# First expert's input by one-hot matmuls, and the third down-projection load behind the second expert's gather

## The chip, the core and the metric

The kernel runs on one core of one Trainium2 chip. The metric is the device time of one execution in microseconds. Engines are named as in the profile: PE is TensorE's matmuls, PEld its weight loads, DVE is VectorE, ACT is ScalarE, POOL is GpSimd, SP is SyncE, and SPq stands for the DMA issues of SP.

## What is computed

Two layers over 512 tokens of width 1024. Each layer is a mixer (attention and retention, then `w_out`) followed by a mixture of 32 experts, two per token; one RMSNorm ends the kernel. The part that matters is the mixture:

```python
g_idx = jnp.argmax(g_logits, axis=-1)              # one of 4 groups per token
top_v, top_i = lax.top_k(e_in_group, K)            # 2 of its 8 experts
eid = (g_idx[:, None] * EXPERTS_PER_GROUP + top_i).reshape(-1)
...
def expert_block(args):
    xblk, e = args
    a = jax.nn.silu(xblk @ w_expert_gate[e]) * (xblk @ w_expert_up[e])
    return a @ w_expert_down[e]
...
out = jax.ops.segment_sum(yb * w_buf[:, None], tok_buf, num_segments=N)
```

Each expert has a gate, an up and a down matrix of 1024x512 or 512x1024 in float32, 2 MB each. All of them are read once per layer, whatever the routing says.

## The kernel before

The 512 tokens are four tiles of 128 rows (`t` = 0 to 3, `NT` = 4). Each expert takes 64 slots (`SLOTS`); a slot holds one token. Rows that do not fit go through further blocks at the layer's end. Each of five engines (SP, POOL, ACT, DVE, PE) runs a program of its own, and semaphores order them. A list of steps (`steps`, line 166) fixes the order in which PE, ACT and DVE go through the mixer and the router; each keeps to that order.

**The end of the mixer and the router.** Step `wo` adds the mixer's output to the residual `xres` (L1320). ACT then takes the sum of squares of the tile (`rstd`, L782, its square at L784). `fT` transposes the tile on PE (L1637), DVE copies it out (L1331), and `lg` makes the 36 router logits (L1644, out of PSUM at L1341). `ffn_rows` (L1015, the multiplication at L1017) writes the normalised tile `xn2[t % 2]` on DVE; for the last tile this comes right behind the last `fT` copy. POOL stores each normalised tile to a DRAM buffer `rows` (L724). `route` (L1069) is a chain of small DVE operations: the choice of the experts (up to L1084), then the rank of each token in its expert, a matmul of PE (steps `rank`, L1651 and L1654), then one-hots of the slots (`hot_slot`, L1100), the weights of the choices (`weigh`, L1052), and, after the matmuls of step `table` (L1455), the list of row numbers `gath` (L1049). `wtab` (L1462) makes the weight of each slot.

**The gathers.** POOL waits for that list and for the four stores, and then issues one indirect DMA per expert (`gather`, L733), which brings the expert's 64 rows into one of three buffers `xg[e % 3]`. The first three go out in a row, each further one as soon as its buffer was transposed.

**The experts.** For each expert PE transposes the gathered rows (L1679), DVE multiplies them by the norm's weight into `xT` (`take_input`, L1351), PE multiplies by gate and up (L1711), ACT applies SiLU, DVE the product (L1354), PE transposes that (L1720), DVE copies it (L1374), PE multiplies by down (L1727), and two more steps (`y_hi`, `y_lo`) and a spreading matmul (L1687) add the result to the residual (L1120). Weights lie in three slots (`RING`). SP issues their loads in one order: expert 3's gate goes out when expert 0's gate matmuls are done, its up after expert 0's up, its down after expert 0's down (`load_expert`, L649), and so on to expert 31. The first three experts are loaded ahead. The last of these nine loads, the down matrix of expert 2, waits in SP's program for the first gather to land (L646):

```python
sp.wait_ge(s_gat[0], 16 * (layer * len(range(0, NE, 3)) + 1))
load_down(layer, 2, 2)
```

and everything that SP issues later, expert 3's gate first, stands behind that wait. `unread` (L1799) is a matmul whose result nobody reads.

## Time and profile before

| | |
|---|---|
| median of 3 runs | 1539.42 us (1537.19 to 1541.54) |
| span of the profiled execution | 1538.5 us; the median lies 0.9 us above it |
| PE busy | 1471.8 us, 96% |
| DVE busy | 822.5 us, 53% |
| ACT, POOL busy | 342.0 us (22%), 262.3 us (17%) |
| mean granted TensorE clock | 0.983 |
| DMA | 464.30 MB, mean 302 GB/s |

The two layers lie one behind the other: mixer and router of layer 0 up to about 306 us, its experts to about 770 us, then the same again. How the page is read: the busy time of an engine is a sum over stages with different limits, so the 96% of PE does not say that PE sets the end. The slices show where DMA is full:

```profile
## 2 busy tenths in 40 slices
PE   8999999799999999998999999996999999999996
...
PEclk9999999799999999999999999997999999999998
DMA  6442144799999999999833321448999999999995
GB/s 205 103 97 69 42 164 178 271 400 423 423 423 421 424 421 423 423 423 424 333 116 95 82 69 28 166 195 350 423 423 422 424 420 425 421 424 421 424 423 228
```

One slice is 38.5 us. In some twenty of the slices, both expert stages, the DMA engines move about 423 GB/s.

### The profile page before, as it was taken

The page shows a single profiled execution, that of the slowest core. Times are in us where ns is not written, and L with a number is a line of the kernel's source. Part 1 is how long each engine was busy: PE and PEld are TensorE (multiplying, and loading weights), DVE is VectorE, ACT ScalarE, POOL GpSimd, SP SyncE. Part 2 cuts the span into 40 slices and gives each one's busy share as a digit, 9 for nine tenths or more (in the row PEclk, how much of TensorE's full clock was granted, in tenths as well). Part 3 has the DMA queues.
Part 4 walks back from the last instruction along what each step waited for, and adds up shares of the span by engine and source line. Part 5 has one row for each costly group of instructions (what it writes and reads, how often), then busy time and mean ns, then how long its engine had stood idle before and what let it go on. Part 6 is the DMA issues. An engine that isn't in the chain of part 4 may idle for free.

```text
span 1538.5 us, 23362 instructions
## 1 busy us (share of the span) xinstructions
PE 1471.8 (96%) x9302; PEld 930.0 (60%) x9302; DVE 822.5 (53%) x1518; ACT 342.0 (22%) x682; POOL 262.3 (17%) x155
## 2 busy tenths in 40 slices
PE   8999999799999999998999999996999999999996
PEld 6877768655555555544488777685555555554443
DVE  2267774545555555454534586635455555555446
ACT  6335463100000000000163354710000000000002
POOL 3343332100000000000133332401000000000001
PEclk9999999799999999999999999997999999999998
DMA  6442144799999999999833321448999999999995
GB/s 205 103 97 69 42 164 178 271 400 423 423 423 421 424 421 423 423 423 424 333 116 95 82 69 28 166 195 350 423 423 422 424 420 425 421 424 421 424 423 228
DMA packets 105932, 464.30 MB, mean 302 GB/s; under 512 B 16706, under 2 KB 59970, under 8 KB 72800
## 3 DMA queue, kind: packets, MB, share of 16 engines
q1 hardware_dynamic: 98208, 449.13, 73.1%
q0 software_dynamic: 6272, 12.60, 2.2%
q8 instruction: 77, 1.26, 0.3%
q10 hardware_dynamic: 1344, 1.05, 0.2%
q14 instruction: 31, 0.25, 0.0%
HBM read 464.84 MB, written 6.29 MB: 306 GB/s over the span
## 4 chain that ended last, share of the span: by engine, by line
PE 78%; DMA 17%; DVE 3%; issue 1%; ACT 0%; DVEq 0%; ACTq 0%; POOLq 0%
PE bank L1711 23%; DMA area<-in_w_expert_up_dram 16%; PE bank L1727 11%; PE bank L1687 7%; PE bank L1559 5%; PE bank L1564 5%; PE bank L1563 5%; PE bank L1629 2%; PE bank L1631 2%; PE bank L1487 2%; PE bank L1630 2%; PE bank L1488 2%; PE bank L1489 2%; PE bank L1579 2%; PE bank L1601 1%; DVE area L1374 1%
## 5 line engine op out<-in xcount | busy, mean ns | idle before, releaser
L1711 PE MATMUL bank<-area 128*64 128x256 f32 x4096 | 464.0, 383 | 19.1 <-DMA area<-in_w_expert_up_dram 16.8
L1711 PEld LDWEIGHTS bank<-area 128*64 128x64 f32 x4096 | 289.1, 138 | 189.0 <-issue 27.3
L1120 DVE TENSOR_TENSOR xres<-xres,bank 128x512 f32<-128x512 f32 x512 | 316.4, 679 | 5.2 <-PE bank L1687 5.2
L1727 PE MATMUL bank<-area 128*64 128x512 f32 x1024 | 233.8, 598 | 6.0 <-DVE area L1374 1.0
L734 POOL DMA_INDIRECT area<-rows,gath x64 | 72.0, 1125 | 746.5 <-PE bank L1679 714.7
L1354 DVE TENSOR_TENSOR area<-area,bank 128x256 f32<-128x256 f32 x64 | 27.0, 421 | 293.3 <-PE bank L1711 293.3
L708 POOL TENSOR_TENSOR w_lo<-area,w_hi 128x1024 fp32r<-128x1024 f32 x55 | 135.1, 2459 | 274.6 <-ACT w_hi L806 274.6
L970 ACT ACTIVATE y_hi<-bank,slot_w 128x512 fp32r<-128x512 f32 x64 | 44.1, 688 | 576.7 <-PE bank L1727 576.7
L1727 PEld LDWEIGHTS bank<-area 128*64 128x64 f32 x1024 | 67.8, 136 | 130.8 <-issue 109.6
L1559 PE MATMUL bank<-h_hi,w_hi 128*128 128x512 f32 x336 | 135.0, 402 | 0.0
L1564 PE MATMUL bank<-h_hi,w_lo 128*128 128x512 f32 x320 | 124.9, 390 | 0.0
L1563 PE MATMUL bank<-h_lo,w_hi 128*128 128x512 f32 x320 | 124.7, 390 | 0.0
L1687 PE MATMUL bank<-y_hi,onehot 64*128 64x512 f32 x512 | 115.6, 446 | 3.0 <-issue 1.6
L1687 PE MATMUL bank<-y_lo,onehot 64*128 64x512 f32 x512 | 102.5, 394 | 0.0
L1687 PEld LDWEIGHTS bank<-y_hi,onehot 64*128 64x128 f32 x512 | 48.4, 184 | 83.5 <-issue 75.8
L966 ACT ACTIVATE area<-bank 128x256 f32<-128x256 f32 x64 | 24.6, 385 | 278.2 <-PE bank L1711 278.2
L1358 DVE SCALAR_TENSOR_TENSOR y_lo<-bank,slot_w,y_hi 128x512 fp32r<-128x512 f32 x64 | 48.0, 750 | 69.9 <-ACT y_hi L970 69.9
L806 ACT ACTIVATE w_hi<-area 128x1024 fp32r<-128x1024 f32 x58 | 61.6, 1062 | 84.0 <-PE bank L1489 32.7
L1559 PEld LDWEIGHTS bank<-h_hi,w_hi 128*128 128x128 f32 x336 | 63.0, 188 | 22.9 <-issue 10.3
L1564 PEld LDWEIGHTS bank<-h_hi,w_lo 128*128 128x128 f32 x320 | 60.1, 188 | 13.0
L1563 PEld LDWEIGHTS bank<-h_lo,w_hi 128*128 128x128 f32 x320 | 60.1, 188 | 11.5
L1374 DVE COPY area<-bank 128x256 f32<-128x256 f32 x64 | 27.2, 425 | 68.6 <-PE bank L1720 68.6
(186 smaller groups left out, 1662.1 us busy)
## 6 DMA issues: line engine op xcount, KB each, us to landing
area<-in_w_expert_up_dram SPq DMA_DIRECT2D x64, 2048.0 KB, 27.4
area<-in_w_expert_gate_dram SPq DMA_DIRECT2D x64, 2048.0 KB, 25.8
area<-in_w_expert_down_dram SPq DMA_DIRECT2D x64, 2048.0 KB, 26.6
area<-in_w_in_dram SPq DMA_DIRECT2D x58, 512.0 KB, 3.9
area<-in_w_out_dram SPq DMA_DIRECT2D x4, 2048.0 KB, 11.1
rows<-area POOLq DMA_DIRECT2D x8, 512.0 KB, 6.2
area<-in_decay_dram SPq DMA_DIRECT2D x2, 1024.0 KB, 6.2
out_dram<-area SPq DMA_DIRECT2D x4, 512.0 KB, 2.9
```

The source lines that it names most:

```text
L708: nc.gpsimd.tensor_tensor(w_lo[g % CUT][:, :, :], slab[g % RAW], w_hi[g % CUT][:, :, :].bitcast(F32), ALU.subtract).then_inc(s_wlo, 1)
L734: pool.indirect_dma_start(out=xg[e % 3], out_offset=None, in_=rows_dram, in_offset=bass.IndirectOffsetOnAxis(ap=gath[:, e:e + 1], axis=0), ...
L806: nc.scalar.activation(w_hi[g % CUT][:, :, :], slab[g % RAW], ACT.Copy).then_inc(s_whi, 1)
L970: nc.scalar.activation(y_hi[e % 2][:, :], bank[3][:, :], ACT.Copy, scale=slot_w[:, e:e + 1]).then_inc(s_yh, 1)
L1120: tt(xs, xs, bank[4 + i][:, :], ALU.add).then_inc(s_sa[i], 1)
L1358: return nc.vector.scalar_tensor_tensor(out=y_lo[e % 2][:, :], in0=bank[found][:, :], scalar=weight, in1=y_hi[e % 2][:, :].bitcast(F32), o ...
L1559: mm(o[:, :], hi[:, c, :], h_hi[:, c, :], start=(c == 0), stop=False)
L1563: mm(o[:, :], hi[:, c, :], h_lo[:, c, :], start=False, stop=False)
L1564: last = mm(o[:, :], lo[:, c, :], h_hi[:, c, :], start=False, stop=(c == KC - 1))
L1687: yield mm(bank[4 + 2 * (t % 2) + half][:, :], onehot[parity][rows, P * t:P * (t + 1)], part[rows, :], start=(w_ == 0), stop=(w_ == 1))
L1711: last = mm(bank[i][SLOTS * half:SLOTS * (half + 1), 0:256], xT[:, c % 4, c // 4, :], w[:, i, c, 256 * half:256 * (half + 1)], start=(c == ...
L1727: last = mm(bank[into][SLOTS * half:SLOTS * (half + 1), :], hx[:, c % 2, c // 2, :], w[:, c, 512 * half:512 * (half + 1)], start=(c == 0), ...
```

## The change

The input of the first expert of each layer no longer comes by a gather. All four normalised tiles are kept in SBUF (`XN0` has four places, and the buffers of the expert stage are laid out around them). Once the ranks are known DVE makes a one-hot per tile for expert 0 (`hot_first`), and PE multiplies it with the kept tiles in a new step `xb`, 8 calls of float32 matmuls. DVE waits for all four stores to land, copies the result to `xg[0]` in two halves, and PE transposes it (`first_transpose`). The gathers begin at expert 1. The list of row numbers is made around the first transposes: 3 matmuls ahead of them, 5 behind; DVE takes the list out of PSUM after it has made expert 0's `xT`. The matmuls of the slot weights move behind expert 0's up matmuls, the weights' DVE work and `further` likewise move into expert 0.

The last normalised tile is written by ACT instead of DVE, after the last logits are complete. ACT no longer waits for a store ahead of the tiles 2 and 3, and its squares go to another scratch place. PE gets `unread` matmuls of 2816 columns in all behind the last `lg`. On SP the down matrix of expert 2 waits for the gather of expert 1.

```diff
@@ -66,15 +66,15 @@
-XN0 = PT0
-XG0 = PB0
-XT0 = XG0 + 3 * 512
-SG0 = XT0 + 512
+XN0 = (PT0, PT0 + D, PB0, PB0 + D)
+YH0 = PB0
+XT0 = YH0 + 4 * 512
+OH0 = XT0 + 512
+SG0 = OH0 + 2 * T
-YH0 = HX0 + 256
-OH0 = YH0 + 4 * 512
-assert PLEN <= (RH - 1) * T and OH0 + 2 * T <= AREA and DK0 + RH * T <= 2 * EXPERT and KT0 + FH * T <= EXPERT
+XG0 = HX0 + 256
+assert PLEN <= (RH - 1) * T and XG0 + 3 * 512 <= AREA and XN0[1] + D <= CS0 and DK0 + RH * T <= 2 * EXPERT and KT0 + FH * T <= EXPERT
...
@@ -224,7 +224,7 @@
-    out += [("fT", 3, 1), ("lg", 3, 1), ("rank",), ("table",), ("wtab",)]
+    out += [("fT", 3, 1), ("lg", 3, 1), ("rank",), ("xb",), ("table",), ("wtab",)]
...
@@ -525,6 +527,11 @@
+        def gathered(layer, e):
+            count = [len(range(i or 3, NE, 3)) for i in range(3)]
+            return 16 * (layer * count[e % 3] + e // 3 + (e % 3 > 0))
...
@@ -641,9 +648,7 @@
-                sp.wait_ge(s_gat[0], 16 * (layer * len(range(0, NE, 3)) + 1))
+                sp.wait_ge(s_gat[1], gathered(layer, 1))
...
@@ -721,14 +726,13 @@
-                    pool.dma_start(dst, xn2[t % 2].rearrange("p (h n) -> p h n", h=2)).then_inc(s_rows[t % 2], 16)
-                pool.wait_ge(s_ret, RH * (layer + 1))
-                nc.gpsimd.memset(at(XG0, 3 * 512), 0.0).then_inc(s_xgz, 1)
+                    pool.dma_start(dst, xn2[t].rearrange("p (h n) -> p h n", h=2)).then_inc(s_rows[t], 16)
+                nc.gpsimd.memset(at(XG0 + 512, 2 * 512), 0.0).then_inc(s_xgz, 1)
-                for i in range(2):
-                    pool.wait_ge(s_rows[i], 16 * (NT // 2) * (layer + 1))
+                for t in range(NT):
+                    pool.wait_ge(s_rows[t], 16 * (layer + 1))
...
@@ -736,7 +740,7 @@
-                for e in range(RING):
+                for e in range(1, RING):
...
@@ -940,10 +944,14 @@
-                        if t >= 2:
-                            act.wait_ge(s_rows[t % 2], 16 * (layer * (NT // 2) + t // 2))
-                        rstd(xres[:, t, :], t, xn2[t % 2], s_rstd2)
+                        rstd(xres[:, t, :], t, at(CS0, D), s_rstd2)
+                    elif kind == "lg" and s[1:] == (NT - 1, 1):
+                        t = s[1]
+                        act.wait_ge(s_rstd2, layer * NT + t + 1)
+                        is_full(act, s[:2], layer)
+                        nc.scalar.activation(xn2[t].rearrange("p (h j q) -> p h j q", h=2, j=4),
+                                             xres[:, t, :].rearrange("p (q h j) -> p h j q", h=2, j=4), ACT.Copy,
+                                             scale=stat[:, 16 + t:17 + t]).then_inc(s_xn2, 1)
...
@@ -958,8 +966,6 @@
-                act.wait_ge(s_tab, layer + 1)
...
@@ -1094,20 +1100,24 @@
+                link(nc.vector.tensor_copy(rank_first, rank[:, :, 0]))
+                for t in range(NT):
+                    ts(hot_first[:, t, :], k("slot")[:, 0:SLOTS], rank_first[:, t:t + 1],
+                       chosen[:, t, 0:1].bitcast(F32), ALU.is_equal, ALU.mult).then_inc(s_first_hot, 1)
-                weigh(layer)
-                b, n = result(("table",), layer)
-                rows_of(layer, ("table",), 0, NE).then_inc(freed[b], 1)
-                for i in range(2):
-                    dve.wait_ge(s_rows[i], 16 * (NT // 2) * (layer + 1))
-                is_taken(dve, ("table",), layer)
-                dve.sem_inc(s_tab, 1)
+                for t in range(NT):
+                    dve.wait_ge(s_rows[t], 16 * (layer + 1))
+                b, n = result(("xb",), layer)
+                is_full(dve, ("xb",), layer)
+                for half in range(2):
+                    own = slice(256 * half, 256 * (half + 1))
+                    nc.vector.tensor_copy(xg[0][:, own], bank[b][:, own]).then_inc(freed[b], 1)
...
@@ -1330,8 +1340,6 @@
-                        if t == NT - 1 and half:
-                            ffn_rows(layer, t)
...
@@ -1370,11 +1378,17 @@
+                    if e == 0:
+                        slot_weights(layer)
+                    if e == 0:
+                        is_taken(dve, ("table",), layer)
+                    if e == 0:
+                        further(layer)
...
@@ -1390,9 +1404,10 @@
-                slot_weights(layer)
-                further(layer)
+                b, n = result(("table",), layer)
+                rows_of(layer, ("table",), 0, NE).then_inc(freed[b], 1)
+                weigh(layer)
...
@@ -1462,6 +1477,10 @@
+            def unread(b, *widths):
+                for n in widths:
+                    mm(bank[b][:, 0:n], ident, kst[:, 0:n], start=True, stop=True)
...
@@ -1654,12 +1673,13 @@
-                    elif kind == "table":
-                        pe.wait_ge(s_tabin, layer + 1)
-                        last = table(o, hot_exp, NE, TOPK * layer)
-                    elif kind == "wtab":
-                        pe.wait_ge(s_wtin, layer + 1)
-                        last = weight_table(o[:, 0:NE], hot_w)
+                    elif kind == "xb":
+                        pe.wait_ge(s_xn2, NT * (layer + 1))
+                        for t in range(NT):
+                            pe.wait_ge(s_first_hot, NT * layer + t + 1)
+                            for half in range(2):
+                                last = mm(o[SLOTS * half:SLOTS * (half + 1), :], hot_first[:, t, :],
+                                          xn2[t][:, 512 * half:512 * (half + 1)], start=(t == 0), stop=(t == NT - 1))
...
@@ -1670,11 +1690,35 @@
-                pe.wait_ge(s_tab, layer + 1)
+                    if s == ("lg", NT - 1, 1):
+                        is_taken(pe, ("lg", NT - 2), layer)
+                        unread(2, 512, 512, 512, 512, 512, 256)
+                def slots_by_expert(part):
+                    b, n = result(("table",), layer)
+                    if part[0] == 0:
+                        may_fill(pe, ("table",), layer)
+                        pe.wait_ge(s_tabin, layer + 1)
+                    last = table(bank[b], hot_exp, NE, TOPK * layer, part)
+                    if part[-1] == TOPK * NT - 1:
+                        last.then_inc(full[b], 1)
+                def weights_by_expert():
+                    b, n = result(("wtab",), layer)
+                    may_fill(pe, ("wtab",), layer)
+                    pe.wait_ge(s_wtin, layer + 1)
+                    weight_table(bank[b][:, 0:NE], hot_w).then_inc(full[b], 1)
+                def first_transpose():
+                    b, n = result(("xb",), layer)
+                    for j in range(4):
+                        if j % 2 == 0:
+                            pe.wait_ge(freed[b], 2 * n - 1 + j // 2)
+                        last = tr(bank[0][:, P * j:P * (j + 1)], xg[0][:, P * j:P * (j + 1)], ident)
+                    last.then_inc(s_xtf, 1)
-                    pe.wait_ge(s_gat[e % 3], 16 * (layer * per(e % 3) + e // 3 + 1))
+                    pe.wait_ge(s_gat[e % 3], gathered(layer, e))
...
@@ -1742,6 +1786,8 @@
+                    if e == 0:
+                        weights_by_expert()
...
@@ -1760,7 +1806,9 @@
-                input_transpose(0)
+                slots_by_expert(range(0, 3))
+                first_transpose()
+                slots_by_expert(range(3, TOPK * NT))
```

## Rows read from the trace of the kernel before

**Rows 1.** Chain of waits, in order of time: start us, us, what.
```profile
602.18 7.08 PE bank L1711 x64
609.28 40.09 DMA area<-in_w_expert_up_dram
```
**Rows 2.** Busy time by stretch, for DMA: window, length, busy per engine, clock, DMA share, GB/s.
```profile
600.00:700.00 100.00, 93.32 (x694) 50.58 (x692) 48.91 (x86) 7.51 (x14) 6.86 (x6) 1.00 1.01 423
...
313.30:315.70 2.40, 2.40 (x26) 1.57 (x24) 1.82 (x5) 0.38 (x1) 0.00 (x0) 1.00 0.66 137
...
1071.80:1074.00 2.20, 2.20 (x24) 1.44 (x22) 1.81 (x5) 0.38 (x1) 0.00 (x0) 1.00 0.76 164
```
**Rows 3.** Timeline of SP, both layers: start us, us, issue.
```profile
305.77 0.38 SPq L595 DMA_DIRECT2D area<-in_w_expert_down_dram  x1
313.64 0.33 SPq L587 DMA_DIRECT2D area<-in_w_expert_gate_dram  x1
...
1064.28 0.38 SPq L595 DMA_DIRECT2D area<-in_w_expert_down_dram  x1
1071.78 0.33 SPq L587 DMA_DIRECT2D area<-in_w_expert_gate_dram  x1
```
**Rows 4.** DMA issues of rows 3, same order, last number us to landing.
```profile
area<-in_w_expert_down_dram SPq DMA_DIRECT2D x1, 2048.0 KB, 9.0
area<-in_w_expert_gate_dram SPq DMA_DIRECT2D x1, 2048.0 KB, 8.9
...
area<-in_w_expert_down_dram SPq DMA_DIRECT2D x1, 2048.0 KB, 8.7
area<-in_w_expert_gate_dram SPq DMA_DIRECT2D x1, 2048.0 KB, 7.8
```
**Rows 5.** The stores of L724: the one at 291.67 us, and all eight.
```profile
rows<-area POOLq DMA_DIRECT2D x1, 512.0 KB, 9.8
...
DMA to landing us min/median/max: 3.2/6.2/10.2
```
**Rows 6.** Timeline of DVE, both layers.
```profile
290.22 1.14 DVE L1017 TENSOR_SCALAR area<-xres,stat 128x1024 f32<-128x1024 f32 x1 [0.23 <-ACT stat L791]
...
298.58 1.29 DVE L1100 TENSOR_TENSOR hot_slot<-kst,area 128x512 fp32r<-128x512 f32 x2
...
301.32 0.25 DVE L1049 TENSOR_SCALAR gath<-bank,kst 128x32 int32<-128x32 f32 x1 [0.30 <-PE bank L1455]
...
301.58 0.42 DVE L1108 COPY area<-nfe 128x512 f32<-128x512 f32 x1
...
307.01 0.69 DVE L1351 TENSOR_TENSOR area<-bank,area 128x512 f32<-128x512 f32 x1 [1.96 <-PE bank L1679]
...
1059.60 0.25 DVE L1049 TENSOR_SCALAR gath<-bank,kst 128x32 int32<-128x32 f32 x1 [0.29 <-PE bank L1455]
```
**Rows 7.** Timelines of ACT and POOL, layer 0.
```profile
288.48 1.06 ACT L784 ACTIVATE area<-xres 128x1024 f32<-128x1024 f32 x1 [14.71 <-DVEq L1324]
...
291.67 0.72 POOL L724 DMA_DIRECT2D rows<-area  x1 [5.27 <-DVE area L1017]
```
**Rows 8.** Timeline of PE, layer 0; last row: L1801's matmul durations, min/median/max ns.
```profile
290.05 1.08 PE L1644 MATMUL bank<-rtw,area 128*128 128x36 f32 x8 [0.88 <-DVE area L1331]
...
318.62 3.65 PE L1727 MATMUL bank<-area 128*64 128x512 f32 x16
...
L1801 PE MATMUL bank<-kst x8: 379/434/697, 765.4 to 771.1; 128*128 128x256 f32 x4, 128*128 128x512 f32 x2, 128*128 128x384 f32 x2
```
**Rows 9.** Busy time by stretch, for the clock: columns as in rows 2, PE first.
```profile
287.61:291.13 3.52, 1.71 (x12) 1.39 (x12) 2.37 (x4) 1.65 (x4) 0.00 (x0) 1.00 1.00 343
291.13:296.40 5.27, 0.01 (x1) 0.02 (x1) 4.58 (x23) 0.00 (x0) 2.12 (x2) 0.55 0.97 405
307.76:312.18 4.42, 4.42 (x22) 2.53 (x24) 3.97 (x14) 0.00 (x0) 1.00 (x1) 0.50 0.96 398
1049.38:1054.70 5.32, 0.00 (x0) 0.03 (x1) 4.63 (x23) 0.00 (x0) 2.12 (x2) 0.51 0.99 415
```

More of the change, by code:

```diff
@@ L272, in banks @@
             b = 5
+        elif kind == "xb":
+            b = 3
         elif kind == "table":
@@ L365, in trunk_kernel @@
         hT2 = [at(PB0 + i * D, D).rearrange("p (c t) -> p c t", c=KC) for i in range(2)]
-        xn2 = [at(XN0 + i * D, D) for i in range(2)]
+        xn2 = [at(start, D) for start in XN0]
         wexp = [(at(s * EXPERT, 2 * KC * DE).rearrange("p (g c n) -> p g c n", g=2, c=KC),
@@ L414, in trunk_kernel @@
         pick = rt(2, TOPK, NT)
+        rank_first = rt(NT)
+        hot_first = rt(NT, SLOTS)
         cmp_st = rt(TOPK * NT, MAXBLK - 1)
@@ L462, in trunk_kernel @@
         s_gate = sem("gate_done")
-        s_sd = sem("decayed_scores_ready")
         s_sq = sem("retention_square_ready")
@@ L469, in trunk_kernel @@
         s_xn2 = sem("ffn_xn_ready")
-        s_rows = [sem(f"rows{i}_saved") for i in range(2)]
+        s_rows = [sem(f"rows{i}_saved") for i in range(NT)]
         s_rtw = sem("router_weights_scaled")
@@ L477, in trunk_kernel @@
         s_hots = sem("one_hots_of_slots_ready")
-        s_tab = sem("tables_ready")
+        s_first_hot = sem("first_expert_one_hots_ready")
         s_wtin, s_wt = sem("slot_weight_one_hots_ready"), sem("slot_weights_ready")
@@ L482, in trunk_kernel @@
         s_more = sem("further_tables_ready")
-        s_wb = sem("ffn_weight_spread")
         s_w = [[sem(f"slot{s}_{n}_loaded") for n in ("gate", "up", "down")] for s in range(RING)]
@@ L1016, in ffn_rows @@
                 dve.wait_ge(s_rstd2, layer * NT + t + 1)
-                ts(xn2[t % 2].rearrange("p (h j q) -> p h j q", h=2, j=4),
+                ts(xn2[t].rearrange("p (h j q) -> p h j q", h=2, j=4),
                    xres[:, t, :].rearrange("p (q h j) -> p h j q", h=2, j=4), stat[:, 16 + t:17 + t], None, ALU.mult
@@ L1447, in _, with table @@
             ident = k("ident")
-            def table(o, hot_col, n, ready=None):
-                for i in range(TOPK * NT):
+            def table(o, hot_col, n, ready=None, part=range(TOPK * NT)):
+                for i in part:
                     if ready is not None and i % NT == 0:
@@ L1495, in _ @@
                     kind = s[0]
-                    if kind in ("gate", "mh", "ml", "ws", "rs") or kind == "fv" and s[1] < 3:
+                    if kind in ("gate", "mh", "ml", "ws", "rs", "table", "wtab") or kind == "fv" and s[1] < 3:
                         continue
@@ L1656, in _ @@
                                       start=False, stop=(u == NT))
-                    elif kind == "table":
-                        pe.wait_ge(s_tabin, layer + 1)
-                        last = table(o, hot_exp, NE, TOPK * layer)
-                    elif kind == "wtab":
-                        pe.wait_ge(s_wtin, layer + 1)
-                        last = weight_table(o[:, 0:NE], hot_w)
+                    elif kind == "xb":
+                        pe.wait_ge(s_xn2, NT * (layer + 1))
[4 more added lines that the diff above has]
+                                          xn2[t][:, 512 * half:512 * (half + 1)], start=(t == 0), stop=(t == NT - 1))
                     if kind == "PV":
@@ L1797, in _ @@
                                 pe.wait_ge(o["added_half"], j * 2 + (part + 1))
-                def unread(b, *widths):
-                    for n in widths:
-                        mm(bank[b][:, 0:n], ident, kst[:, 0:n], start=True, stop=True)
                 if layer + 1 < DEPTH:
```

## The prediction

> **What bounds the kernel now.** I read the slices first, for where DMA is full, then the chain of waits, then the windows at the edges of the full stretch, and last the timelines of the five engines around the router. PE's 96% tempts one to call PE the bound. The chain says something finer: about 22 experts long it runs over PE alone, and from 609.28 us it runs over the loads of the up matrices [rows 1]. From there PE waits for weights. DMA is at full share, 423 GB/s, in that stretch [rows 2], and the slices show the same rate from the first experts on. So the expert stage of a layer ends when one uninterrupted stream of loads ends. At 423 GB/s a 2 MB load takes 4.96 us and an expert 14.9 us, more than PE needs: 7.08 us for gate and up, 3.65 us for down [rows 1, 8] and some 3 us for spreads and transposes. PE starts with three experts loaded ahead and uses that lead up.
>
> The consequence decides this case. **What PE gains at the start of the experts is worth nothing by itself; only an earlier stream is.** The stream of expert 3 to 31 cannot begin before two things in SP's program: the down matrix of expert 2, which waits for a gather, and expert 3's gate, which stands behind it and waits for expert 0's gate matmuls. They were issued at 305.77 and 313.64 us in layer 0, at 1064.28 and 1071.78 us in layer 1 [rows 3]. Between them the stream has a hole: the down matrix landed at 305.77 + 9.0 = 314.8 us, the gate matrix at 313.64 + 8.9 = 322.5 us [rows 4], 7.7 us apart where 4.96 us is the full rate. The hole is 2.7 us by that and (423 - 137) / 423 x 2.4 = 1.6 us by the window [rows 2]; I take 2.2 us. In layer 1 the landings are 1073.0 and 1079.6 us, a hole of 1.6 us, and 1.35 us by the window [rows 2, 4]; I take 1.5 us. The change can win back at most these holes, 3.7 us in both layers, as far as the down matrix is not issued later.
>
> **The change, part by part.** Layer 0, all of it on the way to that issue.
>
> 1. *The last normalised tile moves to ACT.* DVE ended it at 290.22 + 1.14 = 291.36 us and the store went out at 291.67 us, 0.31 us later [rows 6, 7]. Now it waits for the last logits, 290.05 + 1.08 = 291.13 us [rows 8]; ACT starts at about 291.3 us. Its pass over 128x1024 is not in the trace; the nearest are its own square, 1.06 us, and DVE's same strided pass, 1.14 us [rows 6, 7], and up to 1.3 us stays in the range. With 1.06 us the store goes out at 292.65 us, 1.0 us later. It landed after 9.8 us under the weight loads; the bounds are 3.2 and 10.2 us of all eight [rows 5]. With 9.8 us: 302.45 us. What DVE saves is nothing: its logits wait for the same 291.13 us.
>
> 2. *The new wait.* DVE may copy the `xb` result only when all four stores have landed. Behind that wait on DVE stand the copies, `take_input(0)` and the row list, so every gather. Before, the landing at 291.67 + 9.8 = 301.5 us was just hidden behind the list at 301.32 us [rows 5, 6]; now it is last.
>
> 3. *The one-hots and `xb`.* Five small DVE operations ahead of L1100, 0.2 us each by the 0.25 us of L1049 [rows 6], move the end of L1100 from 299.87 to 300.9 us, and the weight copy L1108, 0.42 us, to 301.3 us [rows 6]. `weigh` leaves this place. On PE `xb` is 8 calls of half-width float32 matmuls of 512 columns, just as the down matmuls are: 3.65 us at full clock [rows 8], 7.3 us at half. It starts when the first one-hot is there, about 298.0 us (between PE's restart at 296.40 us [rows 9] and L1100 at 298.58 us [rows 6]), and ends at 301.7 us (300.1 to 302.4 us). Both end before 302.45 us: the store covers them by 0.8 us, and without that cover each microsecond counts.
>
> 4. *From the landing to the list.* Two half copies, 0.4 us each (0.69 us for a full tile in L1351 [rows 6]), 303.3 us; two transposes behind the second, 0.5 us; L1351, 0.69 us [rows 6], then L1049 at about 304.5 us, against 301.32 us: +3.2 us. The five table matmuls in between run beside L1351. Layer 1 has the same chain from its last logits, at 1049.38 us [rows 9]: 1049.38 + 13.4 = 1062.75 us against 1059.60 us [rows 6], +3.2 us.
>
> 5. *Gather and SP.* From L1049 to the issue of the down matrix, 305.77 - 301.32 = 4.45 us and 1064.28 - 1059.60 = 4.7 us [rows 3, 6], stays: it is still the first gather on POOL, only expert 1's. So the down matrix goes out 3.2 us later in each layer, at 309.0 us in layer 0. Queued behind that wait on SP is the whole stream. POOL's clearing of the buffers is shorter and hidden; one gather less falls into a stretch where DMA has room, and saves nothing.
>
> 6. *Expert 0 on PE.* `xT` is ready at 304.6 us, 3.1 us before PE's start at 307.76 us [rows 9]. Even with the old 313.64 - 307.76 = 5.9 us its gate would be done at 310.5 us, and the down matrix keeps the queue full to about 316 us. Expert 3's gate follows without a hole. The slot-weight matmuls now stand between up and down of expert 0 and delay expert 3's down load by some 2 us; it has 5 us of room. `further` on DVE moves behind them and ends before expert 1 needs it. The wait of ACT that is dropped hid nothing.
>
> Sum: layer 0, +3.2 - 2.2 = +1.0 us; layer 1, +3.2 - 1.5 = +1.7 us; together **+2.7 us**.
>
> 7. *The `unread` matmuls.* 2816 columns at 434 ns for one of the two passes of 512 columns [rows 8]: 5.5 x 2 x 0.434 = 4.8 us, from 291.2 to 296.0 us, 0.4 us short of the rank matmuls, if the clock holds at 2.4 GHz. It fell 0.5 us after the last logits in layer 0 and 0.1 us after them in layer 1 (clock means 0.55 and 0.51 [rows 9]); PE had been busy 1.71 of the 3.52 us before that [rows 9], and the change leaves this stretch as it is. In layer 1 I expect it to fall anyway. It came back 4.4 us after the start of dense work in layer 0 [rows 9]; 3.7 us of half clock costs 1.85 us, less 0.4 us of room 1.5 us on the rank, less the 0.8 us of cover from step 3: +0.7 us.
>
> The page TensorE: Matmul & The Clock Gate of the Trainium skill (Part 1) says that the clock is lost after an idle stretch and regained by sustained work; read so, filler without a gap would keep it in both layers and the sum would stay at +2.7 us. The trace speaks against the first half: the clock was gone 0.1 us after PE's last matmul.
>
> Forecast: 2.7 + 0.7 = +3.4 us on the span of 1538.5 us, 1541.9 us; the median lies 0.9 us above the span, so **1542.8 us**.
>
> **The rivals.**
>
> *The store is not last.* Its 9.8 us come from the loads beside it, and a store without them took 3.2 us [rows 5]. Then `xb` at 301.7 us leads, the list comes 2.4 us later instead of 3.2 us, and the sum is +0.2 + 0.9 = +1.1 us, 1540.5 us. For it speaks only that the loads end soon after; against it the 9.8 us itself. The page DMA: Bandwidth & Descriptors (Queues, rings and completion order) has every DMA engine go round between the queues that have work. By an equal share of 423 GB/s 0.5 MB would take 2.5 us, with the page's fixed 2 us an estimate of 4.5 us; the trace has 9.8 us. Chance 0.20.
>
> *The filler costs twice.* The clock falls in layer 0 too, +0.7 to +1.0 us more: 1543.7 us. Chance 0.13.
>
> *Slower: `xb` at half clock.* PE has short gaps between the filler, the rank and `xb`, and all work from 296.4 us to 312.18 us ran at half clock before [rows 9]. Then `xb` takes 7.3 us, ends at 305.3 us, 2.85 us behind the store, and the transposes add 0.4 us: +3.3 us per layer. In both layers the sum is 2.7 + 6.6 = +9.3 us, 1548.7 us; in one, 1545.4 us. It decides from the point where `xb` ends later than 302.45 us; `xb` 2 us later in one layer carries the forecast over the limit below. Against it: the filler ends 0.4 us ahead of the rank. Chance 0.15.
>
> *Faster: the stream is not the bound, or the third down is not last.* Then PE's start counts: expert 3's gate goes out when gate 0 is done, about 304.6 + 3.6 = 308.2 us (half of 7.08 us [rows 1]) instead of 313.64 us, -5.4 us per layer, 1528.6 us. For it: the chain lies on PE to 609 us. Against it: SP cannot issue the gate ahead of the down matrix in its program, and that one waits for a gather which needs the list. Chance 0.07.
>
> *It does not do what it says*: the cut pieces are all hidden and nothing moves, 1539.4 us. Chance 0.05.
>
> **How the numbers follow.** The forecast has 0.40. About 0.3% of the time, 4.6 us, is what a measurement can tell from no change; the limits are 1534.8 and 1544.0 us. Same: most of the forecast (0.34 of 0.40), the first rival, half of the second and the last: 0.66. Faster: 0.06. Slower: the rest, 0.28. The range, 1538.5 to 1548.5 us, goes from the first rival, with 2 us for the holes and the store, to the slow `xb` in both layers; the faster rival and little else lie outside.
>
> **What the changed profile would show.** Right: expert 0's gate matmuls start about 3 us earlier against the last logits, and yet SP issues expert 2's down matrix about 3 us later, expert 3's gate within 0.5 us of it, and the two land 5 us apart. DVE waits for the fourth store with `xb` already done. PE's first wait for an up matrix comes earlier than 609 us while the last loads land 1 to 3 us later. Wrong: the down matrix issued less than 2 us later, or expert 3's gate issued clearly behind it, or PE ending a layer without having waited for weights. A clock at half rate at `xb` would show in its duration.

## The result

The changed kernel takes 1546.31 us in the median of 4 runs (1545.24 to 1549.4), the kernel before 1539.19 us beside it (also 4 runs, one more than in the table above): a ratio of 1.0047, 95% interval 1.0035 to 1.0058. It is slower by 7.1 us; the profiled executions lie 5.7 us apart (1544.2 and 1538.5 us). The forecast was 1542.8 us, +3.4 us.

The page of the changed kernel: busy engines, DMA rate by slice, and the shares of the chain of waits. In what follows the filler is the `unread` matmuls, half clock is a granted TensorE clock of 1.2 GHz, and the stream is the loads from expert 3 on.

```profile
span 1544.2 us, 23483 instructions
PE 1484.3 (96%) x9358; PEld 931.5 (60%) x9358; DVE 824.5 (53%) x1530; ACT 346.1 (22%) x684; POOL 259.5 (17%) x153
...
GB/s 210 98 96 69 42 164 177 259 386 424 421 425 422 423 422 423 423 423 423 333 117 94 82 69 28 171 193 324 424 423 422 423 423 424 421 425 422 424 423 226
...
PE 73%; DMA 23%; DVE 2%; issue 1%; ACT 0%; DVEq 0%; ACTq 0%
```

PE's own busy time grew by 12.5 us: the filler takes 13.1 us and the two `xb` steps 7.3 us, and a higher granted clock (0.992 against 0.983) gives part of it back. What moved is the edge of the full stretch: the slices in which it begins went from 271 and 400 to 259 and 386 GB/s in layer 0, and from 350 to 324 GB/s in layer 1. In the chain of waits DMA's share rose from 17% to 23%. Three pieces of it (start us, us, what):

```profile
293.02 10.68 DMA rows<-area
...
567.76 39.20 DMA area<-in_w_expert_up_dram
...
1055.20 10.43 DMA rows<-area
```

The store of the last normalised tile now stands in the chain of both layers. In the kernel before it was in neither. And PE starts to wait for up matrices at 567.76 us instead of 609.28 us [rows 1], three experts sooner: it is further ahead of the loads than before, and the layer still ends later. A long piece over DMA is a wait for one load that itself stood in the queue behind others; this is how the chain shows a stream.

The timelines of layer 0, by engine: ACT, POOL, DVE, PE, POOL again, SP, and last SP's two issues in layer 1 (start us, us, instruction).

```profile
290.57 2.15 ACT L952 ACTIVATE area<-xres,stat 128x1024 f32<-128x1024 f32 x1 [1.05 <-PE bank L1663]
...
293.02 0.73 POOL L729 DMA_DIRECT2D rows<-area  x1 [7.29 <-ACT area L952]
...
303.92 0.76 DVE L1120 COPY area<-bank 128x256 f32<-128x256 f32 x2 [2.82 <-DMA rows<-area]
305.52 0.69 DVE L1359 TENSOR_TENSOR area<-bank,area 128x512 f32<-128x512 f32 x1 [0.85 <-PE bank L1717]
306.40 0.25 DVE L1055 TENSOR_SCALAR gath<-bank,kst 128x32 int32<-128x32 f32 x1 [0.19 <-PE bank L1470]
...
290.30 6.67 PE L1483 MATMUL bank<-kst 128*128 128x512 f32 x12
296.62 0.42 PE L1670 MATMUL bank<-chosen,sums 128*128 128x160 f32 x1
...
298.13 3.65 PE L1681 MATMUL bank<-area 128*64 128x512 f32 x16 [0.69 <-DVE area L1105]
...
304.40 1.09 PE L1717 MATMUL bank<-kst,area 128*128 128x128 f32 x4 [2.18 <-DVE area L1120]
...
306.30 9.57 PE L1755 MATMUL bank<-area 128*64 128x256 f32 x64
...
307.57 1.28 POOL L738 DMA_INDIRECT area<-rows,gath  x1 [12.86 <-DVE slot_tok L1056]
...
311.10 0.38 SPq L602 DMA_DIRECT2D area<-in_w_expert_down_dram  x1
312.46 0.33 SPq L594 DMA_DIRECT2D area<-in_w_expert_gate_dram  x1
...
1071.70 0.38 SPq L602 DMA_DIRECT2D area<-in_w_expert_down_dram  x1
1072.12 0.47 SPq L594 DMA_DIRECT2D area<-in_w_expert_gate_dram  x1
```

The last logits end at 290.47 us here and at 291.13 us before, at 1052.66 us here and 1049.37 us before in layer 1, so times are compared from there. Expert 0's gate matmuls start 15.8 and 15.2 us behind the logits, against 16.6 and 16.9 us: PE is earlier, by 0.8 and 1.7 us. The down matrix of expert 2 goes out 20.6 and 19.0 us behind them, against 14.6 and 14.9 us [rows 3]: later, by 6.0 and 4.1 us. On DVE the 2.82 us of idle time ahead of the copies is the wait for the store, while `xb` has been complete since 301.78 us.

Two issues of the changed kernel, us to landing: the store at 293.02 us and expert 3's gate matrix at 312.46 us.

```profile
rows<-area POOLq DMA_DIRECT2D x1, 512.0 KB, 10.7
...
area<-in_w_expert_gate_dram SPq DMA_DIRECT2D x1, 2048.0 KB, 13.1
```

Expert 3's gate landed 35.1 us behind the logits, against 31.4 us before [rows 3, 4]; in layer 1 32.7 us, against 30.2 us. These +3.7 and +2.5 us make 6.2 us; the spans differ by 5.7 us. The last load of a layer, the down matrix of expert 31, landed 473.1 and 471.6 us behind the logits, against 469.5 us before in both layers: later by 3.6 and 2.1 us, 5.7 us in all. So the whole difference of the spans is there when the loads end.

### The profile page after: what moved, and what is told of

Same layout as the page of the kernel before. It is cut to its first block, busy times and chain, and to the rows that moved or that the text cites. A ratio compares the mean times of both kernels' runs of the same rounds, so it can differ in the third digit from the quotient of the medians.

```text
span 1544.2 us, 23483 instructions
## 1 busy us (share of the span) xinstructions
PE 1484.3 (96%) x9358; PEld 931.5 (60%) x9358; DVE 824.5 (53%) x1530; ACT 346.1 (22%) x684; POOL 259.5 (17%) x153
## 4 chain that ended last, share of the span: by engine, by line
PE 73%; DMA 23%; DVE 2%; issue 1%; ACT 0%; DVEq 0%; ACTq 0%
DMA area<-in_w_expert_up_dram 21%; PE bank L1755 20%; PE bank L1771 9%; PE bank L1731 6%; PE bank L1578 5%; PE bank L1583 5%; PE bank L1582 5%; PE bank L1648 2%; PE bank L1650 2%; PE bank L1506 2%; PE bank L1649 2%; PE bank L1507 2%; PE bank L1508 2%; PE bank L1598 2%; PE bank L1620 1%; DMA rows<-area 1%
```

## The experiments

The theory (stream): a layer's expert stage ends when the loads of experts 3 to 31 end, and these begin when the down matrix of expert 2 has gone out and expert 0's gate matmuls are done. The rival: PE's start of expert 0 sets the time. Others were on the store, the clock and ACT's pass. All ratios are against the kernel before on the same chip. e1 to e4 ran on one chip, e5 to e7 and e10 on a second, e8 and e9 on a third, so kernels are best compared by their ratios; 0.001 is 1.5 us. The last three columns are worked out from SP's timeline and the landings, in us behind the last logits of the layer: when expert 3's up matrix landed, the second load of the stream, in either layer, and when the last load of the layer landed (layer 0, layer 1).

| kernel | median us | ratio (95%) | up of expert 3, layer 0 | layer 1 | last load |
|---|---|---|---|---|---|
| before | 1539.2 to 1540.5 | 1 | 36.7 | 36.3 | 469.5, 469.5 |
| changed | 1546.31 | 1.0047 (1.0035 to 1.0058) | 40.2 | 37.6 | 473.1, 471.6 |
| e1, last tile on DVE | 1541.72 | 1.0014 (1.0005 to 1.0023) | 36.8 | 36.6 | 469.6, 470.6 |
| e2, third down free | 1538.17 | 0.9992 (0.9983 to 1.0001) | 35.2 | 33.6 | 468.3, 468.2 |
| e3, before, third down free | 1550.33 | 1.0064 (1.0051 to 1.0078) | 40.1 | 40.9 | 472.9, 474.2 |
| e4, no filler | 1547.01 | 1.0051 (1.0037 to 1.0064) | 39.4 | 38.9 | 472.2, 472.2 |
| e5, ACT in order | 1543.71 | 1.0026 (1.0015 to 1.0037) | 37.9 | 38.4 | 471.1, 471.3 |
| e6, list first | 1542.19 | 1.0011 (1.0002 to 1.0021) | 37.8 | 36.9 | 470.3, 469.8 |
| e7, e1 and e2 | 1530.88 | 0.9937 (0.9924 to 0.9951) | 32.1 | 32.0 | 465.8, 465.0 |
| e8, e7 and list first | 1534.81 | 0.9962 (0.9949 to 0.9975) | 31.0 | 31.5 | 465.2, 466.2 |
| e9, e1 and list first | 1538.56 | 0.9990 (0.9979 to 1.0002) | 36.5 | 35.8 | 469.8, 468.7 |
| e10, before, second gather | 1541.27 | 1.0001 (0.9990 to 1.0013) | 37.0 | 36.5 | 469.7, 469.7 |

The last column bears the theory out. Added over both layers, the landing of the last load differs from the kernel before by -8.2 us (e7) to +8.0 us (e3), and in each of the eleven kernels the span of its profiled execution differs by the same to within 1.2 us (e7 by -9.4 us, e3 by +9.2 us). The second load is a rougher sign: in e2 it landed 4.2 us earlier than in the kernel before, added over both layers, and the last load only 2.5 us. Where along the stream such a lead is lost was not traced.

### e1: the last normalised tile back on DVE

```diff
-XN0 = (PT0, PT0 + D, PB0, PB0 + D)
+XN0 = (PT0, PT0 + D, PB0, CS0)
...
-                        nc.scalar.activation(xn2[t].rearrange("p (h j q) -> p h j q", h=2, j=4),
...
+                        if t == NT - 1 and half:
+                            ffn_rows(layer, t)
```

On POOL the clearing of the gather buffers moves behind the landing of the stores and `xb`.

> The changed kernel, but the last normalised tile is written by VectorE again, at its old place right behind the last copy of the transposes; it is kept where the tables of the rotary embedding lie, so GpSimd clears the gather buffers only after the stores have landed and the one-hot matmuls are done. In the changed kernel ScalarE's pass took 2.15 us and began only after the last logits. Theory that this pass and the store behind it set the start of the load stream: the last store goes out 2.0 us earlier against the last logits, lands at about the end of the one-hot matmuls, and everything behind it moves by 1.8 to 2.0 us in each layer: about 4 us off the time of the changed kernel, 1542.5 us. Rival, that the store was not last (the one-hot matmuls or the row list were): VectorE's wait for the store goes away and the time falls by less than 1 us, 1545.5 to 1546.5 us.

Measured 1541.72 us, a ratio of 1.0014 against 1.0047. DVE, PE and SP in layer 0:

```profile
301.97 0.76 DVE L1114 COPY area<-bank 128x256 f32<-128x256 f32 x2 [0.82 <-PE bank L1677]
...
304.00 7.13 PE L1751 MATMUL bank<-area 128*64 128x256 f32 x64 [0.32 <-DVE area L1355]
...
308.54 0.38 SPq L602 DMA_DIRECT2D area<-in_w_expert_down_dram  x1
308.96 0.85 SPq L594 DMA_DIRECT2D area<-in_w_expert_gate_dram  x1
```

DVE's copies now wait for PE, not for the store: the store was last in the changed kernel, and by 2 us. This does not part the two theories, since expert 0 and the down matrix both move earlier. Yet expert 0 now starts 3.1 us earlier behind the logits than in the kernel before (13.5 against 16.6 us), and the kernel is still no faster than it, which speaks for the stream.

### e2: the down matrix of expert 2 free of any gather

```diff
-                sp.wait_ge(s_gat[1], gathered(layer, 1))
                 load_down(layer, 2, 2)
```

> The changed kernel, but the down matrix of expert 2 waits for no gather; SyncE issues it right behind the up matrix of expert 2. Stream theory: the stream of expert 3 on begins when expert 0's gate matmuls are done, with the down matrix already loaded. In the changed kernel expert 3's gate landed at 312.46 + 13.1 = 325.6 us; without the down matrix ahead of it it should take 8.9 us from its issue as in the kernel before, 321.4 us: 4.2 us per layer, 8.4 us in all, 1538 us, although TensorE begins expert 0 no earlier. The first gather, issued after the loads in flight, may be 1 us later at most, which costs nothing. Rival, that TensorE's start of expert 0 sets the time: no change, 1546 us, or later by what the gathers lose.

Measured 1538.17 us, 0.9992. SP and PE in layer 0:

```profile
287.50 0.54 SPq L602 DMA_DIRECT2D area<-in_w_expert_down_dram  x1
311.99 0.33 SPq L594 DMA_DIRECT2D area<-in_w_expert_gate_dram  x1
...
305.65 9.75 PE L1754 MATMUL bank<-area 128*64 128x256 f32 x64
```

PE starts expert 0 15.65 us behind the logits, as in the changed kernel (15.83 us), and expert 3's gate goes out after 22.0 us in both. Only one 2 MB load is gone from between, and the time fell by 8.1 us. The rival has no room for that. This experiment decides it: without the one wait in the title the whole 7.1 us of the change are back. It does not undo an edit of the change, since the kernel before had such a wait too, for the first gather; e3 and e10 try that kernel.

### e3: the same in the kernel before

```diff
-                sp.wait_ge(s_gat[0], 16 * (layer * len(range(0, NE, 3)) + 1))
                 load_down(layer, 2, 2)
```

> The kernel before, with the down matrix of expert 2 free of the gather in the same way. Here the load falls into the time in which expert 0's gather runs. Stream theory: nothing is won, because expert 3's gate already went out as soon as expert 0's gate matmuls were done, with the down matrix landed 1.2 us after that issue; and the gather of expert 0, 3.3 us from issue to landing in the kernel before, now runs beside a load and takes 5 to 10 us as the other transfers beside loads do; expert 0 starts that much later, and the time rises by 2 to 6 us per layer, 1543 to 1551 us. Rival, that the wait protects nothing: the same time, or up to 4 us less if the hole in the stream closes.

Measured 1550.33 us, 1.0064. POOL, PE and SP in layer 0:

```profile
301.85 1.08 POOL L733 DMA_INDIRECT area<-rows,gath  x1 [8.79 <-DVE slot_tok L1049]
...
308.63 1.08 PE L1678 MATMUL bank<-kst,area 128*128 128x128 f32 x4 [4.59 <-DMA area<-rows,gath]
...
316.51 0.33 SPq L587 DMA_DIRECT2D area<-in_w_expert_gate_dram  x1
```

From issue to PE's use the gather takes 6.8 us, against 3.4 us before (302.49 to 305.89 us), beside the load. Expert 0 starts 20.1 and 21.0 us behind the logits, against 16.6 and 16.9 us, and expert 3's gate goes out 3.6 and 4.0 us later. So the wait was worth 10 us where expert 0 needs a gather, and costs 8 us where it does not.

### e4: without the filler

```diff
-                    if s == ("lg", NT - 1, 1):
-                        is_taken(pe, ("lg", NT - 2), layer)
-                        unread(2, 512, 512, 512, 512, 512, 256)
```

> The changed kernel without the matmuls that nobody reads. The clock should be at half rate from the last logits on, as in the kernel before. The one-hot matmuls then take 7.3 us instead of 3.65 us, from about 297.4 to 304.7 us, 1 us behind the landing of the last store at 303.7 us, and the transposes and table matmuls of layer 1 some 0.5 us longer: 1 to 2 us per layer, 1548.5 to 1550.5 us. Rival, that the store covers it all, or that the filler itself is what delays the rank: no change or up to 1 us less, 1545 to 1546.5 us.

Measured 1547.01 us, 1.0051 (1.0037 to 1.0064), below what I expected and not to be told from the changed kernel: the rival holds. In layer 0 `xb` began at 296.68 us, and DVE's wait for the store was 3.22 us:

```profile
296.68 5.00 PE L1681 MATMUL bank<-area 128*64 128x512 f32 x16 [0.70 <-DVE area L1105]
...
302.87 0.76 DVE L1120 COPY area<-bank 128x256 f32<-128x256 f32 x2 [3.22 <-DMA rows<-area]
```

It began at half clock and ended at full clock, a mean granted clock of 0.72 over its 5.00 us, and the store covered it. I had expected half clock throughout. With the store on the path the filler does nothing; what it is worth in e7, where the cover is gone, was not tried.

### e5: ACT's pass in the order of its input

```diff
-                        nc.scalar.activation(xn2[t].rearrange("p (h j q) -> p h j q", h=2, j=4),
-                                             xres[:, t, :].rearrange("p (q h j) -> p h j q", h=2, j=4), ACT.Copy,
+                        nc.scalar.activation(xn2[t], xres[:, t, :], ACT.Copy,
```

> The changed kernel, but ScalarE writes the last normalised tile in the order in which it reads it; the reordering of its columns, which the later stages rely on, is left out, so this kernel does not compute the reference. If the stride of 8 elements on the reading side is what makes the pass 2.15 us, it takes 1.06 us like the square of the same size, the last store goes out 1.1 us earlier and the time falls by 1 us per layer, to 1544.3 us. Rival, that a scale read from memory or the output is what costs: the pass stays at 2.15 us and the time at 1546.3 us.

This kernel leaves out the reordering of the tile's columns and so does not compute the reference; its time and its trace stand. Measured 1543.71 us, 1.0026, 3 us below the changed kernel where 2 us were expected. The pass itself:

```profile
290.34 1.15 ACT L952 ACTIVATE area<-xres,stat 128x1024 f32<-128x1024 f32 x1 [1.46 <-PE bank L1662]
```

Reading out of order, in steps of 8 elements, is the cause of 1.0 of its 2.15 us; the scale and the output were the same in both.

### e6: the row list while DVE waits for the store

```diff
-                slots_by_expert(range(0, 3))
+                slots_by_expert(range(0, TOPK * NT))
                 first_transpose()
-                slots_by_expert(range(3, TOPK * NT))
...
+                b, n = result(("table",), layer)
+                rows_of(layer, ("table",), 0, NE).then_inc(freed[b], 1)
                 for t in range(NT):
                     dve.wait_ge(s_rows[t], 16 * (layer + 1))
```

> The changed kernel, but all eight table matmuls run ahead of the first transposes and VectorE makes the row list before it waits for the last store, in the 2.8 us in which it otherwise idles. Expert 0's input is not earlier (the store still lands at 303.7 us). Stream theory: the first gather goes out about 1 us after the store has landed, at 304.6 us instead of 307.6 us, the down matrix of expert 2 at about 308.2 us instead of 311.1 us, and the time falls by 2.5 to 3 us per layer: 1540.3 to 1541.5 us. Rival, that TensorE's start of expert 0 counts: no change, 1546 us.

Measured 1542.19 us, 1.0011. DVE and SP in layer 0:

```profile
303.34 0.25 DVE L1055 TENSOR_SCALAR gath<-bank,kst 128x32 int32<-128x32 f32 x1 [1.79 <-PE bank L1470]
...
304.29 0.76 DVE L1122 COPY area<-bank 128x256 f32<-128x256 f32 x2 [0.60 <-DMA rows<-area]
...
308.18 0.38 SPq L602 DMA_DIRECT2D area<-in_w_expert_down_dram  x1
312.82 0.33 SPq L594 DMA_DIRECT2D area<-in_w_expert_gate_dram  x1
```

Expert 0 starts 15.66 us behind the logits, as in the changed kernel, and expert 3's gate goes out as late; the down matrix is 3.4 us earlier, and 4.1 us by the medians, 5.5 us by the ratios, are back, where 5 to 6 us were expected. A second time the stream moved and PE's start did not.

### e7: the last tile on DVE and the down matrix free

The edits of e1 and e2.

> The changed kernel with both: the last normalised tile on VectorE, and the down matrix of expert 2 free of any gather. Then the stream begins when expert 0's gate matmuls are done, and these now end 17.2 us after the last logits (with the last tile on VectorE, layer 0) instead of 22.0 us (with only the down matrix free, where the clock fell in between). Stream theory: 2 to 5 us per layer below the 1538.2 us of the free down matrix alone: 1529 to 1534 us, faster than the kernel before by 0.4 to 0.7%. Rival, that the loads in flight delay the last store or the gather of expert 1 so far that this is lost: 1536 to 1539 us.

Measured 1530.88 us, 0.9937 (0.9924 to 0.9951): faster than both kernels, by 0.6% and by 1.0%, and within the 1529 to 1534 us expected. SP and PE in layer 0:

```profile
286.75 0.55 SPq L602 DMA_DIRECT2D area<-in_w_expert_down_dram  x1
308.16 0.33 SPq L594 DMA_DIRECT2D area<-in_w_expert_gate_dram  x1
...
304.44 7.13 PE L1750 MATMUL bank<-area 128*64 128x256 f32 x64 [0.32 <-DVE area L1354]
```

Expert 3's gate goes out 18.2 us behind the logits, against 22.5 us before [rows 3], and lands 8.1 us later with nothing ahead of it. Here at last the earlier start of expert 0 reaches the stream.

### e8 and e9: the list first, in e7 and in e1

The edit of e6 on e7, and on e1.

> The version with the last tile on VectorE and the down matrix free, and in addition the row list ahead of the first transposes. Now nothing of the load stream waits for a gather. Stream theory: the earlier list is worth nothing here, and the five table matmuls and the list stand between the one-hot matmuls and expert 0's input, so that expert 0's gate is done 0.8 to 1 us later: 1.5 to 2 us more than without it, 1532.5 to 1533 us. Rival, that expert 1's gather counts: 1 us less, 1530 us.

Measured 1534.81 us, 0.9962 (0.9949 to 0.9975), where 1532.5 to 1533 us were expected. By the ratios it is slower than e7 by 0.25%, the expected sign, but the two ran on different chips and their intervals just touch. The cause is not settled: expert 3's up matrix landed 1.1 and 0.5 us earlier behind the logits than in e7, not later; the last load came 0.6 us earlier in layer 0 and 1.1 us later in layer 1; and the profiled spans are 1530.1 and 1529.2 us. The profiled execution took 1531.93 us, 2.9 us less than the median, so it does not show what the median has.

> The changed kernel with the last tile on VectorE and the list first, the wait for expert 1's gather kept. The store lands when the one-hot matmuls end, so the list costs expert 0's input 1 us, but the first gather goes out about 0.8 us earlier than with the last tile on VectorE alone (down matrix at 18.0 us behind the last logits). Stream theory: the down matrix goes out at about 17.2 us, the time falls by 1 to 2 us from 1541.7 us, to 1540 us; in no case does it come near the 1530.9 us of the free down matrix. Rival, that expert 0's start counts: 1 to 2 us more, 1543 us.

Measured 1538.56 us, 0.9990 (0.9979 to 1.0002), 3.7 us below e1 by the ratios (3.2 us by the medians), more than the 1 to 2 us expected. The down matrix went out 15.8 and 16.3 us behind the logits, expert 3's gate 19.4 and 18.4 us, so that with the list first it is the gate again that is last. It ends where the kernel before is.

### e10: the kernel before with the wait on the second gather

```diff
-                sp.wait_ge(s_gat[0], 16 * (layer * len(range(0, NE, 3)) + 1))
+                sp.wait_ge(s_gat[1], 16 * (layer * len(range(1, NE, 3)) + 1))
```

> The kernel before, with only the wait changed: the down matrix of expert 2 waits for expert 1's gather instead of expert 0's. Gathers go out 1.35 us apart, so the down matrix goes out 1.3 us later. Stream theory: the load stream of the kernel before has a hole of 1.5 to 2.7 us between this matrix and expert 3's gate, which takes up the 1.3 us: no change, 1539 to 1540 us. Rival, that every delay of this load comes through to the end: 2.6 us more, 1542 us.

Measured 1541.27 us, but its own kernel before gave a ratio of 1.0001 (0.9990 to 1.0013): no change. In layer 0:

```profile
306.46 0.38 SPq L595 DMA_DIRECT2D area<-in_w_expert_down_dram  x1
312.88 0.33 SPq L587 DMA_DIRECT2D area<-in_w_expert_gate_dram  x1
```

Behind the logits the down matrix goes out at 16.1 us (14.6 us before) and the gate at 22.5 us in both. The hole took the 1.5 us. So the words "waits for the second expert's gather" cost nothing by themselves; the cost is that this gather has come to be issued 4.4 us later in layer 0 (307.57 us against 303.87 us, 17.1 against 12.7 us behind the logits; 3.3 us later in layer 1), and that the down matrix waits for a gather at all where expert 0 needs none (e2).

## Why the prediction was right, and where it was short

*The bound and the direction: right.* The argument that only the stream counts, and that the third down matrix is ahead of it, gave slower where PE's gain spoke for faster. e2 and e6 show it: 8 and 4 us back with expert 0 starting as in the changed kernel.

*The size: too small, and inside the range partly by luck.* The kernel is 7.1 us slower where 3.4 us were forecast. I had called "same" the most likely (0.66), and all four runs lie above its limit of 1544.0 us; slower had 0.28. The upper part of the range was there for `xb` at half clock in both layers. That did not happen, `xb` took 3.65 us in both; other terms, which follow, carried the time up there.

*Step 1, ACT's pass: mis-sized, the largest miss.* I took 1.06 us from ACT's square of the same size; it took 2.15 us. The store went out 2.55 us behind the logits instead of 0.54 us, 2.0 us later where the sum had 1.0 us. My range ended at 1.3 us. Neither row had what counted: ACT's 1.06 us is a pass in order, DVE's 1.14 us another engine's. The Trainium skill says, on the page SBUF — State Buffer (Door 1: The DMA port swizzle), that consecutive accesses run at full bandwidth only within one line of 16 bytes; here each step is 32 bytes. ACT's two durations (2.15 and 1.15 us, e5) agree with it. What DVE pays is open, as no run has its pass in order. Its nearest row in the kernel before is a multiplication in order over half as many elements:

```profile
L1279 DVE TENSOR_SCALAR area<-area,rowsum 128x512 f32<-128x512 f32 x16 | 7.8, 487 | 0.6
```

Twice that, an estimate of 0.97 us, is less than the 1.14 us, so DVE may pay something too.

*Step 1, the landing: short.* 9.8 us was forecast, 10.7 and 10.4 us measured: 0.9 and 0.6 us.

*Step 2, the new wait: right.* DVE idled 2.82 and 2.84 us for the store. The first rival, that the store is not last, fell; e1 shows what lies under it, 2 us per layer.

*Steps 3 and 4.* `xb` ran from 298.13 to 301.78 us, forecast 298.0 to 301.7 us. From the landing to the list it took 2.7 us, not 2.05 us: the transposes ran at half clock (1.09 us), and so did the five table matmuls (1.23 us), which I had beside L1359 and for which the list waited another 0.19 us. In all the list came 5.7 us later behind the logits in layer 0 (306.40 - 290.47 = 15.9 us, against 10.2 us), not 3.2 us: 1.0 us by the pass, 0.9 us by the landing, 0.6 us by the clock. In layer 1, with transposes of 0.77 us, it was 4.9 us.

*Step 5: right in layer 0.* List to down matrix 4.70 and 3.96 us, forecast 4.45 and 4.7 us: in layer 1 it was 0.7 us shorter.

*The holes: right.* The down matrix was 6.0 and 4.1 us later, the next load 3.7 and 2.5 us; the holes took 2.3 and 1.6 us, forecast 2.2 and 1.5 us. e10 shows one by itself.

*Step 6: right in what matters.* Expert 0 started only 0.8 and 1.7 us earlier, not 3.1 us, for the reasons above; it hid the gate behind the down matrix as forecast, closely in layer 1 (issued 0.42 us behind it), less so in layer 0 (1.36 us, because the gate matmuls ran at half clock there; I had said within 0.5 us).

*Step 7, the filler: wrong in two ways that cancelled.* Windows of the changed kernel with the filler, from `xb`'s end to the gate matmuls, and the gate matmuls (columns as in rows 9, the clock third from the end):

```profile
290.47:296.97 6.50, 6.50 (x15) 2.93 (x14) 5.43 (x26) 2.42 (x3) 1.69 (x2) 0.74 1.02 427
...
301.78:306.30 4.52, 2.34 (x14) 2.14 (x13) 1.45 (x3) 0.00 (x0) 0.00 (x0) 0.80 0.25 103
306.30:312.30 6.00, 6.00 (x35) 3.52 (x36) 1.35 (x7) 0.00 (x0) 3.31 (x3) 0.58 0.29 70
```

The clock fell to 1.2 GHz inside the filler in layer 0 too, though I had expected it only in layer 1 (the second rival; I had given it 0.13): a mean of 0.74 over 6.5 us is 3.4 us of half clock, and the filler took 6.67 us instead of 4.8 us. In layer 1, where the clock had fallen 0.6 us before the last logits ended, it took 6.42 us. The 3.7 us of half clock that I had put into the sum stood on no row; 3.4 us is what layer 0 shows. The rank came 0.9 and 0.5 us later behind the logits than before, and none of that mattered, since the later store covered it: the +0.7 us of the sum was 0. A second fall, which I had not priced, came in layer 0 at about 304.5 us, at the end of PE's 2.2 us of waiting for the store, and made expert 0's gate and up matmuls 9.57 us instead of 7.13 us. The down matrix covered most of that.

Sum against the spans: forecast +3.4 us, measured +5.7 us. Take from the forecast the 0.7 us for the filler, and add what came out otherwise: +2.0 us for ACT's pass in the two layers, +1.5 us for the landings, +0.6 us for the half clock of layer 0, +0.25 and -0.7 us in step 5, and -0.2 us for the holes. That is 6.2 us, the lateness of expert 3's gate matrix in both layers; of it 5.7 us are left where the last loads land.

The medians lie 7.1 us apart. Most of the remaining 1.4 us lies in which executions were profiled. In every run that has both, the time is 1.8 to 2.5 us above the span, 2.0 us in the mean; by that (an estimate) the profile of the kernel before, 1538.5 us, is of an execution of about 1540.5 us, 1.3 us above its median, and the changed kernel's is one of 1546.12 us, 0.2 us below its median.

## What to carry to other kernels

Ask of a faster start which transfer it lets go out earlier, and read the issuing queue in its own order: a wait there holds all that stands behind it, and when what it waits for moves, the wait has to be judged again. The same edit, that one wait taken out, cost 10 us in the kernel before (e3), and gave 8 us in the changed kernel (e2) and about 11 us on top of e1 (e7). A pass moved to another engine is priced from a row of that engine with the same access pattern, not only the same size.

## What the runs showed of the hardware that I had not expected

- ACT's copy of 128x1024 float32 took 2.15 us (2146 to 2150 ns) reading with a stride of 8 elements and 1.15 us in order; DVE took 1.14 to 1.26 us for the same strided read.
- An indirect gather of 64 rows in halves took 3.4 us from issue to use while the loads ahead of it ran out (360 GB/s in its first us, 94 to 111 GB/s after it), and 6.8 us beside one more 2 MB load (367 to 434 GB/s, e3). The last store of a layer, 0.5 MB under the weight loads, took 9.7 to 10.9 us in all of these kernels, against 3.2 us for one without them [rows 5].
- TensorE's clock fell to 1.2 GHz within the filler of layer 0, while PE was busy without a gap (mean granted clock 0.74 over 6.50 us, PE busy 6.50 us). What lay ahead of it was a stretch with gaps at full clock, 1.71 us busy of 3.53 us:

```profile
286.94:290.47 3.53, 1.71 (x13) 1.50 (x14) 1.46 (x3) 1.65 (x4) 0.00 (x0) 1.00 1.00 354
```

  What made it fall is open: no run varied that stretch.
